# Scores of a differential attention: one four-pass fp32 product over 64 rows, or two fp32r products (128 rows and 64 rows)

## The reference, cut to what matters

```python
qkv = hn @ w_qkv                                   # 512 x 3072
q = apply_rope(q.reshape(B, S, 2 * H, d), cos, sin)   # 8 heads, 2 components each, d = 64
k = apply_rope(k.reshape(B, S, 2 * H, d), cos, sin)
s = jnp.einsum('bqhcd,bkhcd->bhcqk', q_blk, k) * scale
s = jnp.where(causal_mask(i, S), s, -jnp.inf)
p = jax.nn.softmax(s, axis=-1)
a = p[:, :, 0] - lam * p[:, :, 1]
o = jnp.einsum('bhqk,bkhe->bqhe', a, v)
```

## Time and profile before

| | us |
|---|---|
| median of 3 runs | 1815.59 |
| the profiled execution | 1815.4 |
| its span, first to last instruction | 1813.6 |
| PE busy with matmuls | 1798.5 (99%) |
| DVE busy | 879.3 (48%) |
| ACT busy | 623.8 (34%) |
| POOL busy | 537.5 (30%) |
| first attention with its own projection, PE's L782 from | 68.1 |
| to | 207.3 |

### The profile page before, as it was taken

One profiled execution on the slowest core, in us unless ns is written; L12 is line 12 of the kernel. 1 busy time (PEld: TensorE's weight loads), 2 busy tenths in 40 slices (PEclk: granted clock), 3 DMA queues, 4 the chain that ended last, 5 costly groups with the idle time before them and its releaser, 6 DMA issues.

```text
span 1813.6 us, 21898 instructions
## 1 busy us (share of the span) xinstructions
PE 1798.5 (99%) x8496; PEld 1461.5 (81%) x8496; DVE 879.3 (48%) x1223; ACT 623.8 (34%) x916; POOL 537.5 (30%) x340
## 2 busy tenths in 40 slices
PE   9999999999999999999999999999999999999999
PEld 8877788888888887788888888877677888888877
DVE  6556563333334767553333334479655432333357
ACT  4344532222222345422222224334645332221244
POOL 1222254132325530153232225423222220210232
PEclk9999999999999999999999999999999999999999
DMA  6322222222322234325222322322122222232222
GB/s 214 109 80 79 73 93 93 93 93 93 106 95 99 80 106 134 108 93 128 93 95 94 113 93 92 118 74 70 55 93 96 93 93 93 93 116 87 99 95 92
DMA packets 37058, 177.71 MB, mean 98 GB/s; under 512 B 4568, under 2 KB 11512, under 8 KB 18040
## 3 DMA queue, kind: packets, MB, share of 16 engines
q1 hardware_dynamic: 35808, 175.06, 28.4%
q10 hardware_dynamic: 1176, 1.63, 0.7%
HBM read 161.99 MB, written 3.67 MB: 91 GB/s over the span
## 4 chain that ended last, share of the span: by engine, by line
PE 88%; DVE 7%; ACT 2%; issue 1%; POOL 1%; SPq 0%; DMA 0%; DVEq 0%; ACTq 0%; POOLq 0%
PE ps L562 23%; PE ps L563 22%; PE ps L564 22%; PE ps L618 4%; PE ps L607 4%; PE ps L608 4%; PE ps L820 1%; PE ps L782 1%; PE ps L831 1%; DVE idx_score L2210 1%; DVE wlo L1738 1%; DVE top L2208 1%; PE ps L630 1%; PE ps L1000 1%; PE ps L1010 1%
## 5 line engine op out<-in xcount | busy, mean ns | idle before, releaser
L1738 DVE TENSOR_TENSOR wlo<-raw,whi 128x2048 fp32r<-128x2048 f32 x133 | 325.8, 2450 | 301.7 <-ACT whi L1237 301.3
L562 PE MATMUL ps<-xb,whi 128*128 128x512 f32 (+1 forms) x996 | 388.4, 390 | 1.4 <-ACT probs L1541 0.7
L564 PE MATMUL ps<-xb,wlo 128*128 128x512 f32 (+1 forms) x996 | 386.0, 388 | 0.0
L563 PE MATMUL ps<-xb,whi 128*128 128x512 f32 (+1 forms) x996 | 386.0, 388 | 0.0
L1237 ACT ACTIVATE whi<-raw 128x2048 fp32r<-128x2048 f32 x143 | 272.9, 1909 | 324.9 <-PE ps L564 249.2
L562 PE MATMUL ps<-xa_hi,whi 128*128 128x512 f32 x788 | 308.5, 391 | 0.7 <-ACT probs L1306 0.7
L564 PE MATMUL ps<-xa_hi,wlo 128*128 128x512 f32 x788 | 306.8, 389 | 0.0
L563 PE MATMUL ps<-xa_lo,whi 128*128 128x512 f32 x788 | 306.7, 389 | 0.0
L562 PEld LDWEIGHTS ps<-xb,whi 128*128 128x128 f32 x996 | 187.0, 188 | 43.6 <-issue 4.9
L564 PEld LDWEIGHTS ps<-xb,wlo 128*128 128x128 f32 x996 | 187.0, 188 | 38.6
L563 PEld LDWEIGHTS ps<-xb,whi 128*128 128x128 f32 x996 | 187.1, 188 | 37.4
(11 more groups left out here) (332 smaller groups left out, 2427.1 us busy)
## 6 DMA issues: line engine op xcount, KB each, us to landing
raw<-wst SPq DMA_DIRECT2D x148, 1024.0 KB, 4.9
stage<-qk_raw SPq DMA_DIRECT2D x32, 128.0 KB, 2.3
mla_qn<-q_nope SPq DMA_DIRECT2D x8, 256.0 KB, 2.7
mla_v<-v_tok SPq DMA_DIRECT2D x8, 256.0 KB, 2.7
outT<-h SPq DMA_DIRECT2D x7, 256.0 KB, 2.0
h<-xT SPq DMA_DIRECT2D x3, 512.0 KB, 6.8
bias_scratch<-bias_rows ACTq DMA_DIRECT2D x1, 1536.0 KB
raw<-wst SPq DMA_DIRECT2D x4, 256.0 KB, 5.2
```

The source lines that it names most:

```text
L562: pe.matmul(out, lhs_hi, rhs_hi, start=first, stop=False)
L563: pe.matmul(out, lhs_hi, rhs_lo, start=False, stop=False)
L564: return pe.matmul(out, lhs_lo, rhs_hi, start=False, stop=last)
L1738: dve.tensor_tensor(wlo[slot][:, :], raw[slot][:, :], whi[slot][:, :].bitcast(F32), ALU.subtract).then_inc(wlo_done, 1)
```

## The change

The scores are made of fp32r products. ACT rounds roped q and k to fp32r (`qk_high`), DVE subtracts to get the low parts (`qk_low`), both for two 512-wide tiles in one instruction. `stage` for a component now holds q high on both halves of the 128 partitions, and k high on the component's own half with k low on the other: one 128-row matmul gives q high by k high plus q high by k low. `stage_lo` holds q low; a 64-row matmul adds q low by k high. Row tile 0 is made 256 columns wide. The two parts of S(n, i) are: two 128-row matmuls (one a component), then two 64-row ones.

POOL keeps one add of rope, DVE takes the other. `stage_diff` issues 12 DMAs a head (8 of 32 partitions by two rows of 512, 4 by one row; head 6 is split in q and k parts). Buffers move: `qk` takes all 32 KB of `xb`, `pT` goes into the second half of `probs`. `turn` now stands ahead of S(n + 1, 3), and one wait on DVE and two on ACT are changed to fit the buffers.

```diff
@@ -86,6 +86,10 @@
 SWAP = QKV_STEPS[CHUNK_BANKS[5:].index(0)] - 6
...
+QK_HI, QK_LO = (0, 4, 4, 8), (8, 12, 8, 12)
+STAGED = 16 * 12
 def head_chunk(n):
@@ -232,11 +236,16 @@
-        qk_raw = [at(f"qk_raw{j}", [P, 2, 2, S], F32, xb_at + (16 + 8 * j) * K) for j in range(2)]
...
+        qk = at("qk", [P, 16, S], F32, xb_at)
         v_tok = at("v_tok", [P, QT, D], F32, G)
-        stage = [at(f"stage{s}", [P, 2, S], F32, G + (16 + 4 * s) * K) for s in range(2)]
...
+        stage = [at(f"stage{s}", [P, 4, S], F32R, G + o * K) for s, o in enumerate((16, 44))]
+        stage_lo = [at(f"stage_lo{s}", [P, S], F32R, G + o * K) for s, o in enumerate((62, 52))]
         probs = [at(f"probs{s}", [P, 2, ROWLEN], F32, G + (24 + 10 * s) * K) for s in range(2)]
-        pT = [at(f"pT{s}", [P, ROWLEN], F32, G + (44 + 5 * s) * K) for s in range(2)]
+        pT = [at(f"pT{s}", [P, ROWLEN], F32, G + (29 + 10 * s) * K) for s in range(2)]
         o_raw = [at(f"o_raw{s}", [P, QT, P], F32, G + (54 + 2 * s) * K) for s in range(2)]
...
         rope_even, rope_odd = at("rope_even", [P, S], F32, rstd_at), at("rope_odd", [P, S], F32, sq_at + 2 * K)
@@ -366,6 +375,9 @@
         stage_full = [sem(f"stage_full{s}") for s in range(2)]
+        rope_odd_done = sem("rope_odd_done")
+        qk_hi_done = sem("qk_hi_done")
+        qk_lo_done = sem("qk_lo_done")
         mla_full = [sem(f"mla_full{s}") for s in range(2)]
...
         rope_lo = sem("rope_lo")
@@ -458,17 +470,39 @@
-            def stage_diff(n):
+            def stage_diff(n, what="qk"):
...
                 pair, par = n // 2, n % 2
-                sp.wait_ge(rope_done, 2 * pair + 2)
-                if pair:
+                hi, lo = QK_HI[pair], QK_LO[pair]
+                def part(slots, comp, own, hf, src):
+                    rows = 64 * (comp if own else 1 - comp) + 32 * hf
+                    from_rows = slice(32 * (2 * par + comp), 32 * (2 * par + comp) + 32)
+                    dst = stage_lo[par][rows:rows + 32, :] if slots is None else stage[par][rows:rows + 32, slots, :]
+                    sp.dma_start(dst.bitcast(F32), qk[from_rows, src, :]).then_inc(stage_full[par], 16)
...
+                if pair and "q" in what:
                     sp.wait_ge(score_done, 8 * (n - 1))
-                for comp in range(2):
-                    for hf in range(2):
-                        rows = slice(32 * (2 * par + comp), 32 * (2 * par + comp) + 32)
-                        sp.dma_start(stage[par][64 * comp + 32 * hf:64 * comp + 32 * hf + 32, :, :],
-                                     qk_raw[pair % 2][rows, hf, :, :]).then_inc(stage_full[par], 16)
+                if what != "k":
+                    sp.wait_ge(qk_lo_done, 2 * pair + len(what))
+                else:
+                    sp.wait_ge(qk_hi_done, 2 * pair + 2)
+                for own in (True, False):
+                    if what == "k" and not own:
+                        sp.wait_ge(qk_lo_done, 2 * pair + 2)
+                    for comp in range(2):
+                        for hf in range(2):
+                            q, k = hi + 2 * hf, (hi if own else lo) + 2 * hf + 1
+                            if what == "qk":
+                                part(slice(2 * comp, 2 * comp + 2), comp, own, hf, slice(q, k + 1, k - q))
+                            elif what == "q":
+                                part(2 * comp, comp, own, hf, q)
+                            else:
+                                part(2 * comp + 1, comp, own, hf, k)
+                if "q" in what:
+                    for comp in range(2):
+                        for hf in range(2):
+                            part(None, comp, True, hf, lo + 2 * hf)
...
                 sp.dma_start(h[:, 2 * i:2 * i + 2, :], x_view[:, 2 * i:2 * i + 2, :]).then_inc(x_loaded[i], 16)
@@ -499,8 +533,9 @@
                 load(n + 7, (n + 7) % 2)
+            stage_diff(6, "q")
             load(13, 1)
-            stage_diff(6)
+            stage_diff(6, "k")
             stage_diff(7)
...
             load_pairs(C["dkv"] + 2, C["wo_b"] + 2)
@@ -766,7 +801,7 @@
                 if i == 0:
-                    pe.wait_ge(stage_full[n % 2], 64 * (n // 2 + 1))
+                    pe.wait_ge(stage_full[n % 2], STAGED * (n // 2 + 1) + (16 * 8 if n == 6 else 0))
                 if (n, i) == (0, 0):
...
                         pe.wait_ge(bank_free[comp], CHUNK_USE[4] + 1)
@@ -776,11 +811,14 @@
                         pe.wait_ge(score_free[comp], 4 * n + i)
-                q = slice(P * i, P * i + P)
+                q, w = slice(P * i, P * i + P), max(P * (i + 1), 2 * P)
+                st = stage[n % 2]
+                for comp in range(2):
+                    pe.matmul(ps[banks + comp][:, 0:w], st[:, 2 * comp, q], st[:, 2 * comp + 1, 0:w], start=True, stop=False)
                 for comp in range(2):
                     rows = slice(64 * comp, 64 * comp + 64)
-                    pe.matmul(ps[banks + comp][:, 0:P * (i + 1)], stage[n % 2][rows, 0, q],
-                              stage[n % 2][rows, 1, 0:P * (i + 1)], start=True, stop=True).then_inc(score_done, 1)
+                    pe.matmul(ps[banks + comp][:, 0:w], stage_lo[n % 2][rows, q], st[rows, 2 * comp + 1, 0:w],
+                              start=False, stop=True).then_inc(score_done, 1)
@@ -867,9 +905,9 @@
                 diff_weighted(n)
-                diff_scores(n + 1, 3)
                 if n >= 1:
                     turn(o_raw[(n - 1) % 2], n - 1, X["diff_o"] + n - 1)
+                diff_scores(n + 1, 3)
@@ -1286,13 +1324,27 @@
+            def qk_high(pair, s):
...
+                act.wait_ge(rope_done, 2 * pair + s + 1)
+                act.wait_ge(rope_odd_done, 2 * pair + s + 1)
+                if pair >= 2:
+                    for par in range(2):
+                        act.wait_ge(stage_full[par], STAGED * pair)
+                both = lambda at0: slice(at0 + s, at0 + s + 3, 2)
+                act.activation(qk[:, both(QK_HI[pair]), :].bitcast(F32R), qk[:, both(QK_LO[pair]), :], ACT.Copy).then_inc(qk_hi_done, 1)
...
             hi(2, 0, 2)
...
             hi(4, 0, 6)
+            for s in range(2):
+                qk_high(0, s)
             hi(5, 0, 8)
+            for s in range(2):
+                qk_high(1, s)
             def diff_exp(n, i):
@@ -1336,6 +1388,8 @@
                 c = head_chunk(n)
+                if n == HEADS - 2:
+                    act.wait_ge(stage_full[1], STAGED * 4)
                 if n >= 2:
...
                 if c is not None:
@@ -1366,6 +1420,8 @@
                     diff_copy_o(n % 2, n)
+                if n >= 0 and is_rope(c):
+                    qk_high(c // 3, c % 3)
                 diff_exp(n + 1, 3)
             act.wait_ge(dve_const, 4)
@@ -1852,31 +1908,45 @@
                 pair, s = c // 3, c % 3
-                b, raw_qk = CHUNK_BANKS[c] + u, qk_raw[pair % 2]
+                b, x0, x1 = CHUNK_BANKS[c] + u, QK_LO[pair] + s, QK_LO[pair] + 2 + s
                 if u == 0:
...
                         dve.wait_ge(rope_done, 2 * pair + s)
+                        dve.wait_ge(rope_odd_done, 2 * pair + s)
                     if pair >= 2 and s == 0:
                         for par in range(2):
-                            dve.wait_ge(stage_full[par], 64 * (pair - 1))
+                            dve.wait_ge(stage_full[par], STAGED * (pair - 1))
                 tile_ready(2 * c + u)
                 if u == 0:
-                    dve.tensor_tensor(raw_qk[:, 0, s, :], ps[b][:, :], cos_r[:, :], ALU.mult)
+                    dve.tensor_tensor(qk[:, x0, :], ps[b][:, :], cos_r[:, :], ALU.mult)
                     dve.tensor_tensor(rope_odd[:, :], ps[b][:, :], sin_r[:, :], ALU.mult).then_inc(bank_free[b], 1)
...
                     dve.tensor_tensor(rope_even[:, :], ps[b][:, :], sin_r[:, :], ALU.mult)
-                    dve.tensor_tensor(raw_qk[:, 1, s, :], ps[b][:, :], cos_r[:, :], ALU.mult).then_inc(bank_free[b], 1)
+                    dve.tensor_tensor(qk[:, x1, :], ps[b][:, :], cos_r[:, :], ALU.mult).then_inc(bank_free[b], 1)
+                    for j in range(2):
+                        dve.wait_ge(bank_free[CHUNK_BANKS[c] + j], CHUNK_USE[c] + 1)
+                    dve.tensor_tensor(qk[:, x1, :], qk[:, x1, :], rope_odd[:, :], ALU.add).then_inc(rope_odd_done, 1)
...
+            def qk_low(pair, s):
...
+                dve.wait_ge(qk_hi_done, 2 * pair + s + 1)
+                both = lambda at0: slice(at0 + s, at0 + s + 3, 2)
+                dve.tensor_tensor(qk[:, both(QK_LO[pair]), :].bitcast(F32R), qk[:, both(QK_LO[pair]), :], qk[:, both(QK_HI[pair]), :],
+                                  ALU.subtract).then_inc(qk_lo_done, 1)
...
             lo(4, 0)
+            for s in range(2):
+                qk_low(0, s)
             for u in range(2):
...
                 rope_part(4, u)
+            qk_low(1, 0)
             def diff_min(n, i):
@@ -1947,6 +2017,10 @@
```

(11 more changed lines are left out.)

## The result

| | kernel before | changed kernel |
|---|---|---|
| device time, median | 1815.55 us (1815.06 to 1815.91, 4 runs) | 1835.8 us (1835.07 to 1836.33, 4 runs) |
| profiled execution, span | 1815.4 us, 1813.6 us | 1835.07 us, 1833.3 us |
| granted clock, mean | 1.00 | 0.995 |

The ratio is 1.011, with a 95% interval from 1.0098 to 1.0122. The change is slower by 20 us, where 8 were forecast.

What follows compares the result with a forecast made beforehand. PE was taken to bound the kernel, with two rope rounds through DVE and ACT without slack; 4.6 + 2 x 1.1 + 0.3 + 1.5 - 0.5 = +8.1 us gave 1823.7 us, range 1817.5 to 1828.5.

Steps and rivals of the forecast that it cites:

- What bounds the kernel, and where slack is missing: PE busy 1798.5 of 1813.6 us; DVE and ACT without slack at S(0, 1), S(1, 2) to S(2, 1), S(4, 2) to S(5, 1).
- PE's own cost: Score calls: three passes plus an unchanged 0.39 us for the 64-row pairs; a head gains 0.06 us, eight heads 0.5.
- (b): Score calls: 64-row fp32r pairs run one after the other, +3.5 us, 1827.2 us; chance 0.09.
- (e): Score calls: fp32r scores made in four passes each, 5.1 us a head, +41 us, about 1864 us; chance 0.01.
- The start: Before S(0, 1): chunk 6's load queued behind 24 stage DMAs, ACT late by `qk_high`; +4.6 us, at least +4.0.
- rival (a): After the stall before S(0, 1): the clock falls to half, costing 1.5 us more, 1825.2 us; chance 0.19.
- The changed waits on buffers cost nothing: Changed buffer waits: what they wait for is PE work done in order before, so 0 us.
- The rope steps: Before S(2, 1) and S(5, 1): `qk_high` delays tile 3's exponential by 1.1 us at each, 2.2 us together.
- The +0.3 in step 2: Exponential of tile 0 behind a rope step: 0.8 us cover against 1.1 us of `qk_high`, so +0.3 us.
- Staging of head 6: At S(6, 0): k's stage DMAs land at 182.9 against a start at 181.33; +1.5 us.
- The swap of `turn` and S(n + 1, 3): `turn` ahead of S(n + 1, 3): costs nothing; 0.6 us of a `turn` if its cover were gone.
- Range and chances: Whole kernel: 1817.5 to 1828.5 us; forecast 0.54; slower 0.85, no change 0.12, faster 0.03.

Runs made afterwards that it cites:

- run 5: Kernel before with only the score call rewritten: two 128-row fp32r matmuls and a 64-row fp32r pair per tile, staging untouched; 1813.45 us, ratio 0.9987.
- run 6: As run 5, with the 64-row pair replaced by two matmuls over 128 rows; 1807.47 us, ratio 0.9955.
- run 2: Changed kernel with the load of chunk 6 issued between the stage DMAs of head 0 and head 1; 1834.25 us, ratio 1.01.
- run 3: As run 2, and `qk_high(1, 1)` moved on ACT behind the exponentials of S(0, 0) and S(0, 1); 1830.16 us, ratio 1.0082.
- run 4: Changed kernel with unused filler matmuls in PE's two long gaps, 24 ahead of S(0, 1) and 22 ahead of step 1's transposes; 1833.6 us, ratio 1.0102.
- run 9: Run 8 reordered: chunks 6 and 9 `qk_high` before pT copies, chunk 13's load before head 6's staging, chunks 7 and 10 odd rope adds on DVE; 1822.72 us.
- run 1: Changed kernel with `qk_high(2, 0)` and `qk_low(2, 0)` of chunk 6 moved a step later, to step 1; 1826.7 us, ratio 1.0061.
- run 11: Run 9 with chunk 6's high and low parts put back as in run 8; 1817.17 us, ratio 1.0009 to the kernel before.
- run 8: Changed kernel reordered: chunk 6's load before all stage DMAs, chunk 4, 6 and 9 high parts later, rope's odd add on POOL; 1822.64 us, ratio 1.0041.
- run 7: Changed kernel with q's low part multiplied over 128 rows instead of 64; 1829.7 us, ratio 1.0078.
- run 10: Run 9 with q's low part over 128 rows; 1817.95 us, ratio 1.0011.
- run 12: Run 11 with q's low part over 128 rows; 1811.62 us, ratio 0.9979 to the kernel before.

## Why the prediction was wrong

- **What bounds the kernel, and where slack is missing**: right. What was lost was lost at waits of PE and at the lower clock behind them, in the first attention.
- **PE's own cost**: right for the call of tile 1 (0.75 us measured, 0.76 forecast) and in its reason, that the 0.39 us belongs to the 64-row pairs (runs 5 and 6). A head gains 0.2 us and not 0.06. Tile 2 is part of it: from S(1, 2) to S(1, 3), with the float32 of `weighted` between, run 5 takes 3.07 us and the kernel before 3.28, that is 0.21 less where 0.12 was forecast. Rivals (b) and (e) are out: the 64-row fp32r pair starts together, and the call has the cost of three passes and the way into the pair.
- **The start**: the mechanism was right in each step, the size low. The 24 issues took 16.2 us, 0.675 each and not 0.63, so the load of chunk 6 left at 67.03 instead of 66.1, and S(0, 1) came 5.7 us late instead of 4.6. Runs 2 and 3 confirm both causes, the load behind the stage DMAs and ACT behind `qk_high`.
- **The clock**, rival (a): it came, at 2.6 us and not 1.5. The forecast took half of a first 3 us at half speed; after the stall PE ran at half speed from 77.7 to about 83.5, 5.8 us, and half of that is 2.9. Run 4 gives the price apart from the stall. The Trainium skill ("TensorE: Matmul & The Clock Gate", the section on how this bites in real kernels) makes a fall after an idle gap the rule; these stalls of 5.9 and 7.3 us agree, and this rival should have been the forecast. A gap's length does not settle it, though: behind waits of 1.4 us at S(6, 0) the clock fell in runs 2, 3 and 9 and held in the changed kernel and in runs 1, 4 and 11.
- **"The changed waits on buffers cost nothing"**: this is the step that failed ("what they wait for is PE work that is done in order before"). The place cost 9.6 us where the forecast had 1.1 for the first of its two rope steps, so it makes 8.5 of the 12 us that were missing. The sentence was true of PE's and DVE's changed waits, which show in no list above, and untrue of ACT's in `qk_high(2, 0)`. What that one waits for is not PE work alone, but the 12 DMAs behind it. It could have been worked out from the trace of before:

```profile
97.61 1.13 PE L782 MATMUL ps<-stage 64*128 64x512 f32 x4
99.56 0.69 ACT L1306 ACTIVATE probs<-ps,negmin 128x512 f32<-128x512 f32 x1 [1.25 <-DVE negmin L1888]
```

S(1, 3) ends at 98.7; 12 issues of 0.63 take until 106.3; landing 2.2 us later makes 108.5, and `qk_high` 109.6. The exponential of tile 3, which started at 99.56, is then 10 us late. Measured: it started at 117.08, 9.7 us late against S(1, 3). PE's products covered 2.3 us of that, 7.3 were idle, and the clock cost 2.3 more. Run 1 takes exactly this away and gets 9.1 us back.

- **The rope steps**: the second place, S(4, 2) to S(5, 1), cost 0.95 us for the 1.1 forecast. The first can't be told apart within the 9.6. The +0.3 in step 2 did not come: from S(2, 2) to S(3, 1) the changed kernel takes 15.10 us, before 15.19. The cover was enough.
- **Staging of head 6**: right, 1.4 us for 1.5, with the wait where it was said to be.
- **The swap of `turn` and S(n + 1, 3)**: not free, as far as this can be read. In step 3 S(4, 0) stands ahead of the products of chunk 9, and these take the bank of S(3, 3); there PE waits 1.00 us for the exponential, instead of 0.73 before and 0.61 in run 5. From S(3, 2) to S(4, 1) the changed kernel takes 16.11 us, run 5, whose calls cost the same, 15.68: 0.4 us, near the 0.6 that I gave for a lost cover. No run takes back the swap alone.
- **Range and chances**: the direction held. The range ended at 1828.5 because it was built of the terms I had; a wait that I had declared free was in none of them, and the clock was a rival beside the sum although the sum's own stall brings it about.

## What to carry to other kernels

For every wait that a change adds, write down the last thing it waits for, DMAs with their queue included, and the time at which that is done; put it beside the time at which the waiting instruction was due, and ask what stands behind it on the same engine. A place that is reused in a ring makes such a wait out of a mere copy, and moving the copy by one step can be worth more than everything the change gains; check the move in each queue that it passes, since two of my three reorderings (runs 8 and 9; run 11 was the third) made a new wait. If a small-tile pair of matmuls costs more to enter than it saves, fill the unused rows with data whose product is harmless and keep to one shape. Here that gave 4.8 to 6.1 us three times (runs 7, 10 and 12), and with the order put right it made the changed kernel 0.2% faster than the one before.

## What the runs showed of the hardware

- Going into a pair of 64-row matmuls and back costs 0.39 us a call, for float32 and for fp32r alike: 0.75 us for three passes over 256 columns with it, 0.48 us for four passes without it (runs 5 and 6).
- The clock fell to 0.50 in or behind gaps of PE of 3.1, 4.0, 4.2, 4.5, 5.9 and 7.3 us (runs 4, 2, 9 and 8, and the changed kernel twice) and held at 1.00 through one of 2.0 us (run 3). Gaps of 1.4 us at S(6, 0) came out both ways: 0.50 behind them in the profiled executions of runs 2, 3 and 9, 1.00 in the changed kernel and in runs 1, 4 and 11. What decides is not shown. A fall cost 2.6 us at S(0, 1), 2.3 before S(2, 1) and 1.5 at S(6, 0), on top of the wait.
- Stage DMAs of 64 KB landed 2.0 us after their issue in the median (run 11, from 175 to 184 us) and 4.0 us after it when a 1 MB load had been issued just ahead of them (run 8, from 178 to 190 us).
- DVE's addition of 512 elements with both inputs in SBUF took 1.81 us beside POOL's subtraction, which took 1.28, while `qk_low` with 1024 elements and nothing on POOL took 1.2. With both additions on POOL, the second of chunk 10 ended 2.6 us after DVE's last product (run 8), with one on each engine 1.9 us after it (changed kernel): two engines that take turns were still quicker than one.
